# Output weights of the latent attention by halves of the inputs and between the last heads, w_o in chunks of 512 by 512, and x turned by products with a diagonal

## The reference

```python
def rmsnorm(x, g):                       # the same for rms_norm
    y = x * lax.rsqrt(mean(x * x, axis=-1) + EPS)
    return y * g

# first kind, for l in 0, 1
h = rmsnorm(x, norm_mix_g[l])            # norm 0, 2
...                                      # attention (8 heads), short convolution, pooling, three gates
x = x + merged @ w_o[l]                  # (256, 1024) @ (1024, 1024): "WO"
h = rmsnorm(x, norm_ffn_g[l])            # norm 1, 3
gt, up = split(h @ w_ffn_in[l]);  x = x + (silu(gt) * up) @ w_ffn_out[l]

# second kind, i = 0 (latent attention, 16 heads) and i = 1 (dilated attention)
h = rms_norm(x, norm_mix[i]) * (1 + scale1) + shift1      # norm 4, 6
y = mla_mixer(h, ...)                    # ends in o.reshape(B, S, 1024) @ mla_w_o: "MO"
x = x + gate1 * y
h = rms_norm(x, norm_mlp[i]) * (1 + scale2) + shift2      # norm 5, 7
x = x + gate2 * (square(relu(h @ mlp_w1[i])) @ mlp_w2[i])
```

## Time and profile before

| | |
|---|---|
| median of three runs | 1577.72 us (1576.03 to 1578.23) |
| the profiled execution | 1578.04 us |
| its span, first to last instruction | 1576.2 us |
| TensorE matmuls busy | 97% of the span, 10406 instructions |
| TensorE weight loads busy | 86% |
| VectorE busy | 73% |
| ScalarE busy | 52% |
| mean granted TensorE clock | 0.995 |

### The profile page before, as it was taken

One profiled execution on the slowest core, in us unless ns is written; L12 is line 12 of the kernel. 1 busy time (PEld: TensorE's weight loads), 2 busy tenths in 40 slices (PEclk: granted clock), 3 DMA queues, 4 the chain that ended last, 5 costly groups with the idle time before them and its releaser, 6 DMA issues. The chain is left out here.

```text
span 1576.2 us, 25674 instructions
## 1 busy us (share of the span) xinstructions
PE 1530.2 (97%) x10406; PEld 1359.2 (86%) x10406; DVE 1151.1 (73%) x1501; ACT 820.7 (52%) x1113; POOL 132.2 (8%) x119
## 2 busy tenths in 40 slices
PE   7999999999999999999998899999999999999998
PEld 6999989999799998999987688887788888878887
DVE  6898678785778767778579667777878766776665
ACT  6464444444646444444478654454556555554442
POOL 2150000000114000000014000000111112000000
PEclk9999999999999999999999999999999999999999
DMA  9766366666676636667632347667886765346652
GB/s 327 266 216 204 131 231 230 212 238 243 234 268 210 209 117 234 207 215 277 235 126 86 101 143 278 243 226 210 266 310 234 269 169 197 108 144 217 207 172 102
DMA packets 229908, 327.45 MB, mean 208 GB/s; under 512 B 12216, under 2 KB 187808, under 8 KB 229792
## 3 DMA queue, kind: packets, MB, share of 16 engines
q1 hardware_dynamic: 222728, 315.11, 59.4%
q10 hardware_dynamic: 7064, 10.71, 1.9%
HBM read 316.32 MB, written 9.47 MB: 207 GB/s over the span
## 5 line engine op out<-in xcount | busy, mean ns | idle before, releaser
L1751 DVE TENSOR_TENSOR wparts<-raw,wparts 128x2048 fp32r<-128x2048 f32 (+1 forms) x240 | 545.6, 2279 | 211.4 <-ACT wparts L1263 211.1
L1263 ACT ACTIVATE wparts<-raw 128x2048 fp32r<-128x2048 f32 (+1 forms) x240 | 454.8, 1898 | 127.8 <-PE bank L563 92.8
L561 PE MATMUL bank<-hT,wparts 128*128 128x256 f32 x1216 | 348.7, 287 | 2.2 <-DVE hT L1852 1.5
L562 PE MATMUL bank<-hT,wparts 128*128 128x256 f32 x1216 | 343.9, 283 | 0.0
L563 PE MATMUL bank<-hT,wparts 128*128 128x256 f32 x1216 | 343.9, 283 | 0.0
L561 PEld LDWEIGHTS bank<-hT,wparts 128*128 128x128 f32 x1216 | 233.0, 192 | 6.8 <-issue 5.6
L562 PEld LDWEIGHTS bank<-hT,wparts 128*128 128x128 f32 x1216 | 233.2, 192 | 0.2
L563 PEld LDWEIGHTS bank<-hT,wparts 128*128 128x128 f32 x1216 | 233.1, 192 | 0.0
L561 PE MATMUL bank<-wparts,aT 128*128 128x512 f32 (+2 forms) x568 | 217.8, 383 | 1.8 <-DVE aT L1916 1.3
L561 PE MATMUL bank<-wparts,hT 128*128 128x512 f32 (+2 forms) x592 | 211.5, 357 | 3.4 <-DVE wparts L1751 1.6
L562 PE MATMUL bank<-wparts,aT 128*128 128x512 f32 (+2 forms) x568 | 213.5, 376 | 0.0
(11 more groups left out here) (287 smaller groups left out, 1890.9 us busy)
## 6 DMA issues: line engine op xcount, KB each, us to landing
raw<-in_mlp_w SPq DMA_DIRECT2D x64, 1024.0 KB, 5.5
ada_raw<-in_ada_w SPq DMA_DIRECT2D x96, 512.0 KB, 6.4
raw<-in_w_ffn_in SPq DMA_DIRECT2D x44, 1024.0 KB, 5.6
raw<-in_w_in SPq DMA_DIRECT2D x43, 1024.0 KB, 5.5
raw<-in_dil_w_in SPq DMA_DIRECT2D x64, 512.0 KB, 4.8
raw<-in_w_ffn_out SPq DMA_DIRECT2D x22, 1024.0 KB, 5.1
raw<-in_w_o SPq DMA_DIRECT2D x8, 1024.0 KB, 4.8
biasb<-head_bias ACTq DMA_DIRECT2D x16, 512.0 KB, 6.1
```

The lines of the kernel that those rows point to most:

```text
L561: pe.matmul(dst, held[:, 0, :], streamed[:, 0, :], start=start, stop=False)
L562: pe.matmul(dst, held[:, 0, :], streamed[:, 1, :], start=False, stop=False)
L1263: act.activation(view(whi[c % SPL], c), view(raw[c % RAW], c), ACT.Copy).then_inc(s_hi, 1)
L1751: dve.tensor_tensor(view(wlo[c % SPL], c), view(raw[c % RAW], c), view(whi[c % SPL], c).bitcast(F32), ALU.subtract).then_inc(s_lo, 1)
```

## The change

Three edits. (1) The chunks of w_o and of the latent w_o are 512 inputs by 512 output columns. For w_o the two halves of the inputs follow each other for the first 512 columns, then for the last 512. (2) For the latent w_o the first half of the inputs comes first, for all the columns; its 16 triple products are cut in eight pieces of two triples, one issued in each of the steps 12 to 19 of `latent_heads`, behind the scores and ahead of the transposes. The second half runs behind the heads. (3) There is no `xn`: VectorE scales the identity matrix by `rstd` (128 by 128), and TensorE multiplies blocks of x itself with this diagonal.

```diff
-            xn1 = sb("xn1", [P, TT, D], at=ph)
+            turner1 = sb("turner1", [P, TT, P], at=ph)
...
             for c in range(4):
-                chunk(("WO", l, c), kmajor(A["w_o"][l], 256 * c, 256))
+                out_half, half = divmod(c, 2)
+                chunk(("WO", l, c), kmajor(A["w_o"][l][512 * half:512 * half + 512], 512 * out_half, 512))
...
-                    chunk(("MO", 0, c), kmajor(A["mla_w_o_2"][0], 256 * c, 256))
+                    half, out_half = divmod(c, 2)
+                    chunk(("MO", 0, c), kmajor(A["mla_w_o_2"][0][512 * half:512 * half + 512], 512 * out_half, 512))
...
-                      (3, 4, 5, 6, 7) if e == 5 else (0, 3, 4, 5) if e == 7 else (0, 1, 2, 3, 4, 5) for e in range(8)}
+                      (0, 1, 2, 3, 4, 5, 6) if e == 5 else (0, 3, 4, 5) if e == 7 else (0, 1, 2, 3, 4, 5) for e in range(8)}
...
-        SPLIT_AT = {0: 4, 3: 5, 6: 6}
+        SPLIT_AT = {0: 4, 3: 5, 6: 6, 10: 7, 15: 8}
+        OUT_PIECES = {12: (0, 0, 0), 13: (0, 0, 2), 14: (0, 1, 0), 15: (0, 1, 2), 16: (1, 0, 0), 17: (1, 0, 2), 18: (1, 1, 0),
+                      19: (1, 1, 2)}
...TensorE, norm
-                    return pe.transpose(banks[k][:, P * t:P * t + P], xn[:, t, P * k:P * k + P], ident[:, :])
-
-                pe.wait_ge(s_xn, 2 * e + 1)
+                    return pe.matmul(banks[k][:, P * t:P * t + P], x[:, t, P * k:P * k + P], turner[:, t, :], start=True, stop=True)
+
+                pe.wait_ge(s_turner, 2 * e + 1)
                 for k in TURN_EARLY[e]:
-                    if k == 4:
-                        pe.wait_ge(s_xn2, 2 * e + 1)
                     turn_block(k, 0)
+                pe.wait_ge(s_turner, 2 * e + 2)
                 for k in range(DK):
-                    if k in (0, DK // 2):
-                        pe.wait_ge((s_xn, s_xn2)[k // (DK // 2)], 2 * e + 2)
...TensorE, the first kind's w_o
+                four_for_weights()
                 for c in range(4):
+                    out_half, half = divmod(c, 2)
                     w = weights(("WO", l, c))
-                    if c < 3:
-                        token_major(("WO", l, c), w, 0, 256, hT, 0, DK, first_of=None if c else ("mg", l))
-                        used(("WO", l, c))
-                for t in range(TT):
-                    token_major(("WO", l, 3, t), w, 0, 256, hT, 0, DK, (t,))
-                used(("WO", l, 3), ("WO", l, 3, 1))
-                norm(2 * l + 1, xnf)
+                    wide_half(("WO", l, out_half), ("WO", l, c), w, half, None if out_half else ("mg", l))
+                three_for_weights()
+                norm(2 * l + 1, turnerf)
...TensorE, the latent w_o
+            def latent_out(c, t, k0):
+                half, out_half = divmod(c, 2)
+                if (t, k0) == (0, 0):
+                    latent_weights[c] = weights(("MO", 0, c))
+                nm = ("MO", 0, out_half, t)
+                if (half, k0) == (0, 0):
+                    out_sums[nm] = begin("a" if (out_half, t) == (1, 1) else "w", nm)
+                w = latent_weights[c]
+                for k in (k0, k0 + 1):
+                    at = 4 * half + k
+                    if (out_half, t) == (0, 0):
+                        emptied(pe, ("OT", unitm(0) // 2 + at))
+                    m = mm3(out_sums[nm][:, :], aT[:, :, at, P * t:P * t + P], w[:, :, k, :], at == 0, at == DK - 1)
...
             def wo():
-                for h in range(0, MH, 2):
-                    emptied(pe, ("OT", unitm(h) // 2))
-                for c in range(4):
...
+                for c in (2, 3):
+                    for t in range(TT):
+                        for k0 in (0, 2):
+                            latent_out(c, t, k0)
...
             def end_head(i):
+                if i in OUT_PIECES:
+                    latent_out(*OUT_PIECES[i])
...ScalarE, norm_sums of norms 1, 3 and 5
-                    for t in range(TT):
-                        square(e, t, sq, t, 0, 0, 768)
-                    for t in range(TT):
+                    for q in range(4):
+                        half, t = divmod(q, 2)
...
+                        square(e, q, sq, t, half, 512 * half, 512 * half + 512)
...ScalarE: norm_upper and its calls are gone
-            def norm_upper(e, xn, toks=(0, 1)):
-                for t in toks:
-                    act.wait_ge(s_rstd, RSTD_OF[e] + t + 1)
-                    act.activation(xn[:, t, 512:], x[:, t, 512:], ACT.Copy, scale=rstd[:, (RSTD_OF[e] + t) % 2, 0:1])\
...VectorE, norm
-                dve.tensor_scalar(xn[:, t, 0:512], x[:, t, 0:512], rstd[:, i % 2, 0:1], None, ALU.mult).then_inc(s_xn, 1)
+                dve.tensor_scalar(turner[:, t, :], ident[:, :], rstd[:, i % 2, 0:1], None, ALU.mult)\
+                   .then_inc(s_turner, 1)
...VectorE, w_o: additions of 512 columns of one tile each
-                    xs = x[:, :, 256 * c:256 * c + 256]
-                    dve.tensor_tensor(xs, xs, bk[:, :].rearrange("p (t n) -> p t n", t=TT), ALU.add).then_inc(drain_sem(nm), 1)
+                        xs = x[:, t, 512 * half:512 * half + 512]
+                        dve.tensor_tensor(xs, xs, bk[:, :], ALU.add).then_inc(drain_sem(nm), 1)
...VectorE, the latent w_o
+                        dve.tensor_tensor(y, bk[:, :], gbc0[:, 512 * half:512 * half + 512], ALU.mult).then_inc(drain_sem(nm), 1)
+                        emptied(dve, nm)
+                        xs = x[:, t, 512 * half:512 * half + 512]
+                        dve.tensor_tensor(xs, xs, y, ALU.add).then_inc(s_x2, 1)
```

More of the change, by code:

```diff
@@ L592, in _, with wide_half @@
             wide_banks = {}
-            def wide_half(name, chunk_name, w, half, first_of=None, between=idle):
+            def wide_half(name, chunk_name, w, half, first_of=None, between=idle, a=hT):
                 at = 4 * half
@@ L658, in turn, with norm @@
                 end(m, name)
-            def norm(e, xn):
+            def norm(e, turner):
                 banks = {}
@@ L710, in _ @@
             for l in range(DEPTH):
-                norm(2 * l, xn1)
+                norm(2 * l, turner1)
                 four_for_weights()
@@ L869, in mlp @@
                         ffn_down(("M2", i), c - 1, accs, NF2, 2 * NF1 + NF2 * i)
-            norm(4, xnm)
+            norm(4, turnerm)
             def turn_latent(kp, c):
@@ L962, in _ @@
             mlp(0)
-            norm(6, xnd)
+            norm(6, turnerd)
             four_for_weights()
@@ L1819, in norm @@
                     dve.sem_inc(s_ss, 1)
+                if 0 < ev < 7:
+                    turning_diagonal(ev, turner, 0)
                 norm_mean(ev, 1)
-                if ev in (0, 7):
-                    norm_lower(ev, xn, 0)
-                norm_lower(ev, xn, 1)
+                if ev == 0:
+                    dve.wait_ge(s_const, 16)
+                for t in range(1 if 0 < ev < 7 else 0, TT):
+                    turning_diagonal(ev, turner, t)
             hc, lc = [0], [0]
@@ L2079, in _ @@
                 split_ahead(("AO", l, 1))
[L2080 to L2095 removed]
+                for c in range(3):
+                    split_ahead(("WO", l, c))
+                    if c == 0:
+                        continue
+                    half = c - 1
+                    for t in range(TT):
+                        nm = ("WO", l, half, t)
+                        bk = full(dve, nm)
+                        xs = x[:, t, 512 * half:512 * half + 512]
+                        dve.tensor_tensor(xs, xs, bk[:, :], ALU.add).then_inc(drain_sem(nm), 1)
+                        if (half, t) == (1, 0):
+                            norm_mean(2 * l + 1, 0)
+                norm(2 * l + 1, turnerf)
                 norm_out(2 * l + 1, lambda k: colA[:, c_ffn(l) + k:c_ffn(l) + k + 1])
@@ L2165, in _, with norm2 @@
                 dve.wait_ge(s_bout, BOUT * (l + 1))
-            def norm2(ev, i, which, xn, order=classed):
-                norm(ev, xn)
+            def norm2(ev, i, which, turner, order=classed):
+                norm(ev, turner)
                 norm2_out(ev, i, which, order)
@@ L2251, in mlp @@
                             norm_mean(6, 0)
-            norm2(4, 0, 0, xnm)
+            norm2(4, 0, 0, turnerm)
             split_ahead(("LI", 0))
@@ L2404, in _ @@
             mlp(0)
-            norm2(6, 1, 0, xnd, strided)
+            norm2(6, 1, 0, turnerd, strided)
             second_tile = []
```

118 lines of the change are left out of this document (39 added, 79 removed).

## The result

| | before | after |
|---|---|---|
| median | 1577.91 us (20 runs) | 1580.49 us (20 runs) |
| range of the runs | 1575.1 to 1581.27 | 1576.91 to 1585.98 |
| ratio of the two, 95% interval | | 1.0016 [1.0009, 1.0023] |
| profiled execution, its span | 1578.04, 1576.2 us | 1576.91, 1575.1 us |

The changed kernel is 2.6 us slower, not 4.5 us faster. The profiled execution of after is the fastest of its 20, so its trace looks better than the kernel is.

What follows compares the result with a forecast made beforehand. TensorE, busy 97% of the span, was taken to bound the kernel: its matmuls plus its standstills. Terms -1.1 + 1.3 - 0.6 - 0.1 - 3.5 - 1.0 + 0.4 = -4.6 gave 1573.2 us, range 1567.5 to 1578.

Steps and rivals of the forecast that it cites:

- Price of a block: Turning at the norms: a product with the diagonal takes two passes, 0.23 us a block, 0.43 at 1.2 GHz.
- Norm 0: At the kernel's start: first projection at 14.4 us instead of 12.31; +1.3 us, bounds 0 and +2.
- Norms 6 and 7: Clock may fall as before: -0.7 us for both with it up, +1.7 down; +0.4 taken.
- Norm 5: Behind the latent w_o: longer tail, seven early blocks; -1.8 us with the clock up, +0.4 down; -1.0 taken.
- Norms 2 and 4: Norm 2: shorter idle time keeps the clock up, -0.6 us (+1.0 if it falls); norm 4, clock up: -0.1.
- w_o of layers 0 and 1: 512 columns give -1.0 us, the longer end +0.6, the norm behind gains; -0.55 a layer, -1.1 for both.
- Latent w_o: Pieces partly fill TensorE's idle time among the last latent heads, splits delay the heads; -3.5 us, ends -8.4 and +0.4.
- a tail of +0.75: Between the latent w_o's last matmul and norm 5: gate and add of 512 columns, and the square, +0.75 us.
- (D): Rival: double turning on a slow clock at norms 1 to 7, +8.1 us there; total +5.1, 1583; chance 0.12.
- (B): Rival: products keep the clock up at norms 2, 5, 6, 7, transposes don't; -7.8 us, 1570.2; chance 0.1.
- (A): Rival: pieces fit in idle time, splits delay nothing, clock up at norms 2, 5 to 7; -11.4, 1566.5; chance 0.1.
- (C): Rival: the latent heads stretch by what the pieces take; latent term +0.4, total -0.7 us, 1577.3; chance 0.2.

Runs made afterwards that it cites:

- e10_prod0: Kernel before with both w_o edits, products with the diagonal at norm 0 only, transposes at the other norms; -2.3 us against before.
- second profile: The changed kernel, unchanged, profiled again along with the follow-up experiments; its span is 1578.0 us.
- e9_prod7: Kernel before with both w_o edits, products with the diagonal at norm 7 only, transposes at the other norms; -1.9 us against before.
- e4_wo: Kernel before with only w_o of layers 0 and 1 changed to 512 by 512 chunks; -1.3 us against before.
- e3_mo: Kernel before with only the latent w_o changed (512 by 512 chunks, first half in pieces among the heads); -3.9 us against before.
- e14_mo_late: Kernel before with only the latent w_o edit, but all eight pieces run behind the heads; +1.9 us against before.
- e1_wo_mo: Changed kernel with the old turning back (x scaled in full, 16 transposes a norm), both w_o edits kept; 1575.22 us, -3.6 against before.
- e2_turn: Kernel before with only the turning changed to products of x with the diagonal; 1579.68 us, +0.9 against before.
- e16_turn_again: Kernel before with only the turning changed to products with the diagonal, timed a second time; +1.0 us against before.
- e11_after_warm: Changed kernel plus unread identity transposes in TensorE's idle time ahead of norms 0, 2, 4, 5, 6, 7; -2.3 us against before.
- e12_mo_warm: Kernel before with only the latent w_o edit, plus unread identity transposes ahead of norms 0, 2, 4, 5, 6, 7; -4.2 us against before.

## Why the prediction was wrong

The failed step is the turning behind the longest waits: "Norm 7's 16 blocks follow each other without a pause, 3.7 us instead of 2.8", with +0.4 for norms 6 and 7 as a middle between -0.7 with the clock up and +1.7 with it down. I priced the block rightly and took the full clock for norm 7's. Measured, the two norms cost +0.3 together with the clock up (norm 7's 6.84 against 6.34, norm 6's 7.11 against 7.28) and +3.1 with it down at both (8.36 and 8.38), and the clock was down at norm 7 in both profiles. The windows of before over the idle time at norm 7 and over its turning (columns as in the earlier trace rows) show what I had not asked for:

```profile
1388.80:1391.60 2.80, 0.00 (x0) 0.00 (x0) 2.02 (x7) 2.23 (x7) 1.05 (x2) 1.00 0.00 0
1391.60:1392.90 1.30, 1.23 (x10) 1.06 (x11) 0.57 (x3) 1.15 (x3) 0.07 (x1) 1.00 0.00 0
1392.90:1394.10 1.20, 1.20 (x8) 1.18 (x6) 1.17 (x3) 0.91 (x3) 0.00 (x0) 0.50 0.00 0
```

The clock fell in the middle of the turning, so ten transposes had still run at 2.4 GHz. In after TensorE stood idle for 2.7 us in the same way, the turning had twice the instructions, and 16 of the 32 ran at 1.2 GHz with nothing to cover them. The change lengthened work that sits right behind the longest idle times of the kernel.

*Price of a block.* 0.23 us at the full clock predicted; (919.47 - 915.70) / 31 = 0.122 a pass, 0.24 a block, measured. Two passes: right, 32 instructions a norm. At the low clock the passes start 0.213 us apart, 0.43 a block, as predicted.

*Norm 0.* Right. Projection at 14.04 and 14.49, predicted 14.4; and by the first matmul of w_o, at 175.16 and 175.27 where before had it at 174.13, 1.0 and 1.1 of it are left, predicted 1.3. By e10_prod0 it is 1.3 as well. What was not predicted lies further on in layer 0, between norm 1's projection and norm 2: there TensorE waits 1.1 us (after) and 0.4 (second profile) for VectorE's `h`, before had no such wait.

*Norms 6 and 7.* +0.4 predicted. The gap at norm 7 grew by 2.0 in both profiles, that at norm 6 went from 7.28 to 7.11 in the first and to 8.38 in the second, where the clock fell. Mis-sized by 1.4 to 2.7. e9_prod7 has 1.7 for norm 7 alone.

*Norm 5.* -1.0 predicted; the clock stayed up as hoped, but the gap was 6.96, not 6.35. I had taken seven early blocks as covered by the wait for tile 1. With the new tail both diagonals come together, and nothing is covered. Behind the projection 0.8 came for the predicted 0.7, so the norm gave 0.4 in all instead of 1.0.

*Norms 2 and 4.* Gap 5.38 predicted and measured at norm 2 with the clock at 1.00, and 5.76 at norm 4, where 5.74 stood. But the 0.6 that the full clock behind norm 2's projection should have given does not show: from there to w_o it is 161.2 us before, 161.3 in after and 161.1 in the second profile.

*w_o of layers 0 and 1.* Right. Norm 1's gap 4.69 became 5.22 (+0.53, predicted +0.45). From the first to the last matmul of w_o it is 22.88 us instead of 23.87 in both layers, 1.0 shorter, as predicted. The second chunk waits longer for its split, as said: timeline of PEld of after, answering to the earlier trace rows:

```profile
181.88 0.19 PEld L565 LDWEIGHTS bank<-wparts,hT 128*128 128x128 f32 x1 [1.41 <-DVE wparts L1753]
```

1.41 against 0.71 idle. e4_wo, without the diagonals' share in the term, measured -1.3; by the term's own numbers (-1.0 and +0.6 a layer) it should have been -0.8, within the error.

*Latent w_o.* Predicted -3.5 for the stage; its last matmul came 3.3 earlier relative to norm 4's projection in after, 1.5 in the second profile (both ran 3.4 us at 0.50 in this stretch, from 836.5 and 844.8 us, so the fall by itself does not explain the difference, and it stays open), and e3_mo measured -3.9. The stalls stood where I put them, 1.97 and 1.11 us idle against 1.9 and 1.6. The mechanism, an idle stretch filled in part, was right, and e14_mo_late shows it.

*The sum itself.* By my own terms the two w_o edits were worth -3.6 (-0.4 a layer, -3.5 and a tail of +0.75), and e1_wo_mo measured -3.6. Within the error all of the miss is in what was left for the products, -1.0: on top of these edits they cost 5.8. Single parts gave -4.3 and I forecast -4.6, a nearness without meaning, since the three are not independent: MO's tail takes away the cover under which products are cheap at norm 5. I had worked out the tail and the turning in two terms and never laid them on one time line.

*The rivals.* (D), the slower one, had the right mechanism, a double turning on a slow clock, in the wrong places: I put it at norms 1 to 7, with 1.2 for norm 7, and wanted three more falls of the clock. It took no more falls: norm 7, where the clock was falling already, cost 2.0, and in single traces norm 5 or 6 came on top. I wrote that nothing in the profile spoke for it, and asked only whether the clock would fall more often, not what the falls that were there would now cost. (B) was half right: with products the clock stayed up at norms 2 and 5, and e2_turn and e16_turn_again have a median granted clock of 0.998 against 0.995. The traces say more on (B) than that. Of the 15 without idle transposes, this many show a fall of the clock between the last matmul ahead of a norm and its first projection:

| norm | 2 | 4 | 5 | 6 | 7 |
|---|---|---|---|---|---|
| turned by transposes | 4 of 8 | 5 of 8 | 7 of 8 | 8 of 8 | 8 of 8 |
| turned by products | 0 of 7 | 0 of 7 | 1 of 7 | 3 of 7 | 6 of 7 |

So products do spare the kernel falls at four norms, and pay at norm 7, where they do not. Whether that is because they are products or because the idle time ahead of them is shorter (2.8 instead of 3.0 us from the last matmul to the turning at norm 6) no run separates. (A) and (C) fall: the splits delayed the heads, and the pieces did not stretch them by their own length.

My range ended at 1578 though the bounds added up to 1582.6. I had left out the end that held.

## What to carry to other kernels

Work right behind a long idle time of TensorE should be priced at the lower clock where the trace before shows it fall there: at norm 7 it fell in 14 of 15 traces, and doubled work that costs 0.5 us at the full clock cost 2.0. Before doubling an operation that looks covered, find who waits for whom at its end: here TensorE waited only 0.2 to 0.3 us behind the transposes at norms 0 and 7, and everything beyond that was bare. When a change has several parts that meet at one place, measure them in pairs; the single gains added up to the forecast and the whole was a loss.

## What the runs showed that I had not expected

Transposes that nobody reads keep the clock up. In none of the five profiles with them did the clock fall at a norm. In e11_after_warm twelve of them, TensorE's only work until then, started 0.21 us apart, and the passes behind them 0.11; in after the same passes started 0.21 apart for 5.7 us. The Trainium skill, "TensorE: Matmul & The Clock Gate", Part 4 (PE-mode transpose), says that a transpose does not count as TensorE being busy in the same way and that the full clock does not engage for it. For these fp32 transposes of 128 by 128 the full clock does engage: in e12_mo_warm TensorE had done nothing but transposes when their distance went from 0.21 to 0.11 us, at 10.6 us; the measurement decides. Whether they count less than products the table above leaves open.

At norm 0 the granted clock reads 1.00 while the first 26 passes take 0.21 us each, what they take elsewhere at 0.50. Window over that stretch of after:

```profile
8.20:14.40 6.20, 6.17 (x31) 6.20 (x32) 2.46 (x5) 2.77 (x5) 0.29 (x1) 1.00 1.06 390
```

At the start of a kernel the pace of the instructions tells the clock, the record does not.

A kernel can gain granted clock and lose time: the changed kernel has a median of 0.996 to 0.997 against 0.995 and is slower. By the counts above the clock falls at fewer norms, but there is more work, and norm 0's slow stretch does not enter the figure.
